# Masks loaded in the first feed-forward, the turned memory stored six panels in, and the positions converted in a step of their own

## The reference

```python
# first block, layer l: branches mla, diff and mem, gates, layernorm, feed-forward
cos, sin = rope_tables(positions)            # angle = position * theta**(-2i/rot)
h  = x @ w_in[l]                             # latents (CQ, CKV), dq, dk, dv, gates
kv = mem @ mem_w_kv[l]                       # mem: 256 x 1024; keys and values, 512 wide each
x  = layernorm(ALPHA * x + merged @ w_out[l])
x  = layernorm(ALPHA * x + square(relu(x @ mlp_w1[l])) @ mlp_w2[l])
# second block, layer l: three scans (ssd, hgrn2, mlstm) with triangular masks, feed-forward
```

## Time and profile before

| what | value |
|---|---|
| median of 3 runs | 2543.95 us (2542.56 to 2553.97) |
| the profiled execution's own time | 2551.44 us |
| its span | 2549.6 us |
| granted TensorE clock, mean | 0.988 of 2.4 GHz |
| TensorE busy | 2469.2 us of the span |
| HBM read, written | 424.44 MB, 3.24 MB |

### The profile page before, as it was taken

How to read it: one execution, slowest core, us unless ns; L and a number is a source line. 1 busy time by engine, 2 the same in 40 slices (tenths; PEclk the granted TensorE clock), 3 DMA queues, 4 the chain that set the end, 5 groups by cost and what they waited for, 6 DMA issues and landing times.

```text
span 2549.6 us, 42244 instructions
## 1 busy us (share of the span) xinstructions
PE 2469.2 (97%) x17296; PEld 2263.1 (89%) x17296; DVE 1798.8 (71%) x2929; ACT 1442.8 (57%) x2106; POOL 268.0 (11%) x221
## 2 busy tenths in 40 slices
PE   7999999999999999899999999999999999999998
PEld 6888989988889899799999798998898999898987
DVE  4558675565586765677867897785597768887874
ACT  4646655545466455476555655664666656545654
POOL 0000002000000000001122720000000206500000
PEclk8999999999999999999999999999999999999999
DMA  6553566555544565555456745565554467645664
GB/s 234 162 142 101 161 218 202 182 186 167 139 114 149 170 198 191 177 150 141 123 174 196 196 140 175 182 196 190 154 156 123 140 191 201 184 147 175 192 201 133
DMA packets 358772, 430.44 MB, mean 169 GB/s; under 512 B 20472, under 2 KB 286166, under 8 KB 358324
## 3 DMA queue, kind: packets, MB, share of 16 engines
q1 hardware_dynamic: 341312, 401.72, 51.6%
q10 hardware_dynamic: 14340, 15.91, 2.8%
q0 software_dynamic: 2928, 10.11, 1.3%
HBM read 424.44 MB, written 3.24 MB: 168 GB/s over the span
## 4 chain that ended last, share of the span: by engine, by line
PE 82%; DVE 10%; ACT 4%; issue 2%; DMA 1%; SPq 0%; ACTq 0%; POOL 0%; POOLq 0%; DVEq 0%
PE ps L112 80%; DVE wlo L121 3%; PE ps L115 2%; DVE sE L121 1%; ACT L118 1%; ACT whi L118 1%; DMA wring<-in_mem_w_kv 1%; ACT hgKm L118 1%; ACT E L118 0%; ACT lnv L118 0%; DVE hgQB L121 0%; DMA kT<-in_diff_lambda 0%; DVE hgQF L121 0%; SPq L154 0%; DVE E L124 0%
## 5 line engine op out<-in xcount | busy, mean ns | idle before, releaser
L121 DVE TENSOR_TENSOR wlo<-wring,whi 128x1024 fp32r<-128x1024 f32 (+1 forms) x768 | 920.7, 1219 | 276.6 <-ACT whi L118 276.3
L118 ACT ACTIVATE whi<-wring 128x1024 fp32r<-128x1024 f32 (+1 forms) x768 | 801.6, 1053 | 441.8 <-PE ps L112 410.2
L112 PE MATMUL ps<-uT,whi 128*128 128x256 f32 x4640 | 822.9, 282 | 7.9 <-DVE wlo L121 4.5
L112 PEld LDWEIGHTS ps<-uT,whi 128*128 128x128 f32 x4640 | 708.8, 189 | 17.5 <-issue 8.7
L112 PE MATMUL ps<-uT,wlo 128*128 128x256 f32 x2320 | 647.3, 279 | 0.0
L112 PEld LDWEIGHTS ps<-uT,wlo 128*128 128x128 f32 x2320 | 438.9, 189 | 0.0
L112 PE MATMUL ps<-xT,whi 128*128 128x256 f32 x2112 | 383.8, 285 | 2.4 <-DVE xT L121 1.3
L112 PEld LDWEIGHTS ps<-xT,whi 128*128 128x128 f32 x2112 | 325.6, 190 | 10.2 <-issue 6.3
L112 PE MATMUL ps<-xT,wlo 128*128 128x256 f32 x1056 | 297.0, 281 | 0.0
L112 PE MATMUL ps<-whi,hid 128*128 128x512 f32 x864 | 270.1, 392 | 2.0 <-DVE wlo L121 2.0
L112 PEld LDWEIGHTS ps<-xT,wlo 128*128 128x128 f32 x1056 | 200.9, 190 | 0.3
(11 more groups left out here) (393 smaller groups left out, 3579.3 us busy)
## 6 DMA issues: line engine op xcount, KB each, us to landing
wring<-in_w_in SPq DMA_DIRECT2D x346, 512.0 KB, 4.2
wring<-in_mlp_w SPq DMA_DIRECT2D x128, 512.0 KB, 4.4
wring<-in_w_up SPq DMA_DIRECT2D x88, 512.0 KB, 4.6
wring<-in_w_down SPq DMA_DIRECT2D x44, 512.0 KB, 4.6
wring<-in_w_branch SPq DMA_DIRECT2D x32, 512.0 KB, 3.4
wring<-in_w_out SPq DMA_DIRECT2D x32, 512.0 KB, 4.2
wring<-in_mem_w_kv SPq DMA_DIRECT2D x16, 512.0 KB, 7.3
wring<-in_w_br_hg SPq DMA_DIRECT2D x16, 512.0 KB, 5.6
```

The costliest lines, as they stand in the source:

```text
L112: return self.e.matmul(*p, **k) if self.e else Nothing()
L118: return self.e.activation(*p, **k) if self.e else Nothing()
L121: return self.e.tensor_tensor(*p, **k) if self.e else Nothing()
```

## The change

Masks and small constants become two loads: `load_second` on ScalarE's queue loads only columns C_INV to C_END (32 columns, 16 KB), and `load_rest` on GpSimd's queue loads columns C_U to C_INV (1920 columns, 960 KB) ahead of its wait for a panel. The users of the masks wait for `masks` instead of `consts`. `keep_mem` moves from the place before the keys to the one behind panel 5, and waits for that panel's products instead of the last remainder of `memT`. The conversion of the positions becomes a step of its own, `positions`, behind `load_small` and ahead of panel 5. The order of TensorE's work stays.

```diff
@@ schedule
     do("load_second", xN)
-    do("keep_mem", memT)
     ar.give(memN)
     memkv = [mem_pieces()]
     run(mem_keys(0, memT))
     prow, values = ar.take("prow", 128), mem_values(0, memT)
     some(values, 1)
     do("load_small", prow)
+    do("positions")
+    some(values, 1)
+    do("keep_mem", memT, len(panels) - 1)
     run(values)
     run(turned(xN.tok(), 8, lambda c, t: ["x"], to_pair(xT)))
@@ tensor_program, cumsum_rows
-        e.wait_ge(*at("consts"))
+        e.wait_ge(*at("masks"))
@@ scalar_program, load_second
-        e.dma_start(cst[:, C_U:C_END], a["consts"][:, C_U:C_END]).then_inc(*up("consts", "consts", by=16))
+        e.dma_start(cst[:, C_INV:C_END], a["consts"][:, C_INV:C_END]).then_inc(*up("consts", "consts", by=16))
@@ vector_program
+    def positions():
+        e.wait_ge(*at("posi"))
+        e.tensor_copy(K.posr[:, :], K.posi[:, :]).then_inc(*up("dve_tables", "positions"))
+
     def rope_tables(u):
         chain = "dve_tables"
-        e.wait_ge(*at("posi"))
-        e.tensor_copy(K.posr[:, :], K.posi[:, :]).then_inc(*up(chain, "positions"))
@@ gpsimd_program
     def load_rest(prow, p):
 
+        e.dma_start(K.cst[:, C_U:C_INV], a["consts"][:, C_U:C_INV]).then_inc(*up("masks", "masks", by=16))
         e.wait_ge(*at(("panel", p, 1)))
@@
-    def keep_mem(x):
-        e.wait_ge(*at((x.name, 6)))
+    def keep_mem(x, p):
+        e.wait_ge(*at(("panel", p, 1)))
         e.dma_start(K.memkeep, x.ap).then_inc(*up("memkeep", "memkept", by=16))
```

More of the change, by code:

```diff
@@ L2660, in final_gain @@
         e.tensor_tensor(f.hg.tok(512)[:, t, :], f.h[:, t, 0:512], f.gain.ap[:, 0:512], ALU.mult).then_inc(*up("dve_rows", ("fgain", t)))
-    parts = dict(split_lo=split_lo, rope_tables=rope_tables, lower_bounds=lower_bounds, split_bank=split_bank, split_bank_scaled=split_bank_scaled,
+    parts = dict(split_lo=split_lo, positions=positions, rope_tables=rope_tables, lower_bounds=lower_bounds, split_bank=split_bank, split_bank_scaled=split_bank_scaled,
                  latent_out=latent_out, latent_norm=latent_norm, kpe_out=kpe_out, mla_rope=mla_rope, scores=scores, weights=weights,
```

## The result

| | before | changed |
|---|---|---|
| median of 12 runs | 2544.07 us | 2533.86 us |
| lowest and highest | 2540.26, 2553.97 | 2526.01, 2547.14 |
| profiled execution's span | 2549.6 us | 2530.2 us |
| mean granted clock | 0.988 | 0.991 |

The ratio is 0.9959 with a 95% interval of 0.9945 to 0.9973: 10.4 us faster (6.9 to 14.0), 0.41%. The forecast was 13.5 us. The interval of 6.9 to 14.0 us also holds the forecast 13.5 us, so the times alone can't say that the forecast was too large; that has to come from the profiles.

A forecast was written before the change was run, and what follows sets the result against it. TensorE bounds the kernel, DMA bytes its first stage up to 32 us. Terms 7.3 + 2.7 + 1.8 + 1.7 = 13.5 us off 2543.95 us gave 2530.5 us; own range 2524.5 to 2538 us, 8-in-10 range 2524.5 to 2540.5 us.

The forecast's parts named there:

- The stall ahead of panel 5 goes: TensorE's idle time from 24.84 to 32.16 us goes, 7.3 us, and the low clock after it, 2.7 us.
- The low clock behind the positions: From 47.16 to 51.27 us the clock of 0.58 returns to full once the hole is gone: 1.7 us.
- The positions: Converting them ahead of panel 5 ends TensorE's wait at their transpose; panel 8's products start 1.8 us earlier.
- Panels 6 to 8: Weight panels issued right behind panel 5 land by 26 us, ahead of TensorE's need: no new stall.
- the ring behind the store: Panels 11 to 14 share the DMAs with the moved store and still land in time: cost 0.
- mem_kept: ScalarE's wait for the store's end, about 50 us; the store ends between 33 and 42 us: nothing waits.
- the masks' place: GpSimd issues the masks after 361.13 us, where the DMA share is low: cost 0.
- the small constants: The 16 KB left on ScalarE's queue land before VectorE needs them at 47 us: cost 0.
- The remainder of panel 10 behind the table chain: VectorE finishes it by 51.0 us, where TensorE asks at 50.95 us: a wait of 0 to 0.3 us.
- Rival 1: Part of the stall ahead of panel 5 stays: saving 7.4 us, 2536.5 us; chance 0.15.
- Rival 2: The moved transfers were hidden, the stall coming from small loads or x: saving 3.5 us, 2540.5 us; chance 0.07.
- Rival 3: The moved conversion waits for the positions and blocks VectorE: slower, up to 7.2 us at 46.68 us landing; chance 0.04.

The follow-up runs named there:

- e7: The kernel before with only the 16 small loads moved behind the issue of panel 7: 2542.48 us, ratio 0.9991 (0.9977 to 1.0006).

## Why the prediction was right, and where its sum was off

The measured median, 2533.86 us, lies in the forecast's own range (2524.5 to 2538 us), and the change is within half a per cent of before, to which the text gave 0.49, with 0.48 for a larger gain; the point value was 3.4 us low. The mechanism was right: moving the bytes removed the stall. Three sizes were too large because they were read from one execution, whose stall was the longest of four: the stall, the low clock behind it and the low clock behind the positions. And one small wait was missed.

- **The stall ahead of panel 5 goes**: right. The byte count gave a landing at 22.0 us; the copy started at 20.69 us, early as the text had said of the count, though 0.9 of the 1.3 us are the earlier issue. The size was off: the term took 7.3 us of stall and 2.7 us of low clock from one execution. Over three profiles of before the stall (7.31, 5.71 and 5.63 us) is 6.2 us in the mean, and the products of panels 5 to 7 take 10.6 us where the changed kernel needs 8.4 us, so the low clock is 2.2 us. From the start of panel 4's last product, 24.45 us, to the transposes of x at 42.96 us stood 18.5 us there; over three profiles of before the transposes start at 42.96, 40.57 and 41.55 us, 41.7 in the mean, and in two of the changed kernel at 33.86 and 33.16 us, 33.5 in the mean. The two terms, 10.0 us together, are 8.2 us, or 8.5 us when each profile is counted from its first product of panel 4 (21.93, 21.83 and 22.18 us before, 22.65 and 21.95 us in the changed kernel).
- **The low clock behind the positions**, 1.7 us: wrong as a fixed term. It is worth 0.7 us in the mean if the 3 of 7 executions with the hole are taken, and 1.1 us by the 2 of 3 of before. The text counted a fall that it had seen once as one that comes each time.
- **The positions**, 1.8 us: 1.4 us. Before, 4.20 us pass from the transposes of x to the product of panel 8 (42.96 to 47.16, and 40.57 to 44.77); in the changed kernel 2.81 us. What the step missed is the bank: the transposes of x take the four PSUM banks of their ring in turn, so those of `prow` and of the positions take the first two again, and `bank_free` waits for the first and second remainder of xT. That is the 0.15 and the 0.28 us. The first stood there before as well (45.03 us in the earlier trace rows); the second and the 0.15 us from the positions' transpose to the product are what the forecast left out. The text looked at what the transpose reads and not at where it writes. The run with the tables later fits: with the transpose of the positions out of the way the product starts 0.65 us sooner, and at its later place that transpose shows no wait.
- **Panels 6 to 8, the ring behind the store, `mem_kept`, the masks' place, the small constants**: cost 0, as forecast. The store was issued at 28.73 us, landed after 8.1 us, and even its double was covered. Neither TensorE nor ScalarE waited for a load in the changed kernel between 36 and 60 us.
- **The remainder of panel 10 behind the table chain**: no wait was seen.
- **Rival 1** (part of the stall stays) holds for each part alone, 1.46 us for the store alone and 2.43 us for the masks alone, and not for the change. **Rival 2** (hidden) falls with the store alone, and its other leg, the small loads, with `e7`. **Rival 3** (the conversion blocks VectorE) falls: it found the positions landed at 24.29 us.

In sum 8.2 + 1.4 + 0.7 = 10.3 us, against 10.4 us measured, where the interval of the times is some 3.5 us to either side.

The Trainium skill's rule to issue a DMA early and wait late (DMA: Bandwidth & Descriptors, Rules for kernel authors) says that the fixed setup cost overlaps then. It says nothing of the bytes, and the prediction took it for more when it had the transfers cost nothing by that rule. No run here measures the setup cost. The bytes had a price where the DMA share was about 1.0 (1.03 from 15.39 to 29.79 us): the store, waited for some 35 us after its landing at 28.8 us, cost 5.1 us.

## What to carry to other kernels

In this kernel a store that nobody waited for held back the panel that TensorE waited for, where the DMA share was about 1.0. In such a stretch, count the bytes between the issue and the landing of the late tile, look in the DMA view which queue gets the engines' time, and move those that have a later deadline to a stretch with a low share, still ahead of that deadline. Size a saving from more than one profiled execution: a stall that is made by contention, and a clock that falls after it, differed by some 2 us each between executions of the same kernel here.

## What the runs showed of the hardware

- The same stall, with the same DMAs (before three times, and the positions alone), was 7.31, 5.71, 5.63 and 5.15 us in four executions.
- Between 19.5 and 20.5 us before, three queues moved 16, 16 and 17 packets and 0.26, 0.12 and 0.01 MB. Once alone, the panels' queue moved 0.38 MB in a microsecond.
- After the same 1.68 us without work, behind 1.91 us of transposes, the clock fell in 3 executions and stayed in 4.
- After the stall ahead of panel 5 the clock was 0.84 or less over the products from there to the transposes of x where the stall was 2.43 us (masks alone) or longer, and 1.00 where it was 1.46 us (store alone).
- At a granted clock of 1.00 the products of 128x512 did not always come at the same pace: in the changed kernel 33 steps from product to product lie between 25.92 and 33.62 us, 0.233 us each, and before 23 between 37.70 and 42.96 us, 0.229 us each. No run tells why.
